# x loaded in two halves of 512 features, with the second half transposed behind the second slot of the first projection

## The chip, the core and the metric

The kernel runs on one core of a Trainium2 chip. The metric is device time in microseconds. The engines that this text speaks of are TensorE (PE in the profile), which multiplies; ScalarE (ACT), VectorE (DVE) and GpSimd (POOL), which prepare its operands; and SyncE (SP), which issues the loads. Each runs its own list of instructions in order, and they wait for one another by semaphores.

## What is computed

Two transformer blocks run one after the other on x, 512 tokens of 1024 features. Only the first lines of the first block lie near the change:

```python
def rms_norm(x, gain):
    xf = x.astype(jnp.float32)
    y = xf * lax.rsqrt(jnp.mean(xf * xf, axis=-1, keepdims=True) + EPS)
    return (y * gain.astype(jnp.float32)).astype(x.dtype)

hn = rms_norm(x, norm1_g[l])
proj = hn @ w_in[l]
qa, ka, va = [proj[..., i * WIDTH_A:(i + 1) * WIDTH_A] ... for i in range(3)]
...
x = x + mixed @ w_out[l]
x = x + conv_glu(rms_norm(x, norm2_g[l]), w_ffn_up[l], ...)
```

The projection `qa` sums over all 1024 features. The norm's root is taken of the mean of squares over all 1024 features too.

## The kernel before, in words

**Products in slots.** Every projection is cut into slots. A slot is one block of 128 input features (index k, eight of them in 1024) by 512 output columns. Its weights are one load of 128x512 fp32 into one of four raw buffers (`w_raw`, line 638). ScalarE rounds it to `w_hi` (`hi`, line 897) and GpSimd subtracts to get `w_lo` (`lo`, line 688); there are eight buffers of each. The activations are split likewise: `h_hi` by ScalarE (`first_unscaled`, line 941) and `h_lo` by VectorE (`first_lo`, line 1443). TensorE makes three products for each of four output tiles, twelve matmuls of 128x128 by 128x512 in a slot (line 1693; line 1715 for the first slot). The results of the first projection, qA, gather in banks 0 to 3 of the accumulation memory.

**Loads.** SyncE's queue issues them in order. The load of slot s waits until `w_lo` of slot s-4 is done (line 631 and the wait after it), since both halves of the split read the raw buffer. Behind the loads of slots 4 to 7 stand 18 small loads of gains and the like (lines 606 to 621), five behind each of the first three.

**The start.** x comes as four blocks of 128 tokens (`tb`) by 1024 features, 512 KB each, and then the weights of slots 0 to 3. TensorE transposes each block in eight pieces of 128x128 (`turned`, line 1748), so that feature block j of all tokens stands in bank j. For each j, VectorE or ScalarE copies the bank to `xT` (`first_copied`, lines 1435 and 934), ScalarE makes `h_hi` with the gain (the root is applied only to the outputs), and VectorE makes `h_lo`. ScalarE also squares and sums each block of tokens along the features (`first_square`, line 929), which gives one number per token and block in `xstat`.

**The sum of squares.** VectorE spreads each of the four columns of `xstat` over an identity matrix, in a rounded part and a rest (`sum_hi` line 1477, `sum_lo` line 1478, 128x128 each, eight instructions in all). The step `sumsq` is two matmuls of TensorE over them (lines 1651 and 1652). It stands behind slot 5 of qA in TensorE's order and waits for the last `sum_lo`. Then ScalarE takes the root (lines 952 and 954), and VectorE scales qA by it while copying out (line 1151).

**What sets the order.** `make_schedule` writes one list of steps by hand, and every engine runs through that list and does its part of each step. The number ahead of a step in the plan is the slot behind which it stands: `(5, ("sumsq", 0))`. A step `fill` is the splitting of a slot's weights eight slots ahead. `bank_uses` goes through the same list to count who used which bank before.

## Time and profile before

| | before |
|---|---|
| median of 3 runs | 1571.48 us (1570.23 to 1572.79) |
| span of the profiled execution | 1569.2 us |
| TensorE busy | 1559.0 us, 99% of the span |
| ScalarE busy | 692.7 us, 44% |
| VectorE busy | 643.8 us, 41% |
| GpSimd busy | 754.0 us, 48% |
| HBM traffic | 142.24 MB read, 2.13 MB written, 92 GB/s |

The profiled execution has no time of its own beside the span from its first to its last instruction; the median of the runs lies 2.3 us above that span. A busy share is an average over the whole span. The change touches some thirty microseconds at its start, so the rows further down are nearly all from there, and times in them are microseconds from the start of the span.

### The profile page before, as it was taken

To read this page: it belongs to the slowest core of one execution; us is meant where nothing else is said; L and a number is where in the kernel's file an instruction comes from. 1 tells how busy PE (TensorE), PEld (TensorE's weight loads), DVE (VectorE), ACT (ScalarE), POOL (GpSimd) and SP (SyncE) were. 2 spreads that over 40 slices of the span, in tenths; PEclk is the share of its full clock that TensorE was granted. 3 is DMA by queue.
4 is the path that set the end of the run, shared out by engine and by line. 5 is a ranking of instruction groups with operands and counts; after the bars stand their busy time and mean duration, and the time that the engine had idled before them with its cause. 6 is when DMAs were issued, how large, how long until landed. Compare 5 with 4: busy or idle time off the path is not lost.

```text
span 1569.2 us, 23311 instructions
## 1 busy us (share of the span) xinstructions
PE 1559.0 (99%) x8022; PEld 1258.1 (80%) x8022; DVE 643.8 (41%) x1081; ACT 692.7 (44%) x1194; POOL 754.0 (48%) x577
## 2 busy tenths in 40 slices
PE   8999999999999999999999999999999999999999
PEld 7877777888888888888877887778888888888887
DVE  5344465244355444220488544542442222210234
ACT  5565445334544444332543644754353333322342
POOL 6632475543644454444487433334544444444441
PEclk9999999999999999999999999999999999999999
DMA  5422222222323333333333224222333333333331
GB/s 178 149 74 62 67 68 68 83 86 88 115 86 95 107 100 99 96 97 92 81 95 90 76 66 135 68 68 75 108 94 101 95 99 94 113 95 98 96 94 61
DMA packets 103352, 145.60 MB, mean 93 GB/s; under 512 B 11109, under 2 KB 57166, under 8 KB 103134
## 3 DMA queue, kind: packets, MB, share of 16 engines
q1 hardware_dynamic: 103102, 142.30, 30.9%
q10 hardware_dynamic: 160, 2.11, 0.3%
q8 instruction: 55, 0.90, 0.2%
q14 instruction: 35, 0.29, 0.1%
HBM read 142.24 MB, written 2.13 MB: 92 GB/s over the span
## 4 chain that ended last, share of the span: by engine, by line
PE 97%; DVE 1%; DMA 0%; issue 0%; ACT 0%; SPq 0%; DVEq 0%; ACTq 0%
PE bank L1693 88%; PE bank L1601 2%; PE bank L1630 2%; PE bank L1618 2%; PE bank L1848 1%; DMA xtok<-in_x 0%; PE bank L1679 0%; DVE h_lo L1443 0%; PE bank L1871 0%; PE bank L1888 0%; PE bank L1748 0%; PE bank L1824 0%; PE bank L1882 0%; PE bank L1909 0%; PE bank L1825 0%
## 5 line engine op out<-in xcount | busy, mean ns | idle before, releaser
L688 POOL TENSOR_TENSOR w_lo<-w_raw,w_hi 128x512 fp32r<-128x512 f32 x516 | 697.6, 1361 | 784.8 <-ACT w_hi L897 784.2
L897 ACT ACTIVATE w_hi<-w_raw 128x512 fp32r<-128x512 f32 x516 | 320.0, 630 | 660.8 <-PE bank L1693 590.7
L1693 PE MATMUL bank<-h_hi,w_lo 128*128 128x512 f32 x1244 | 489.0, 393 | 1.5 <-DVE hgate L1159 1.4
L1693 PE MATMUL bank<-h_hi,w_hi 128*128 128x512 f32 x1244 | 484.4, 389 | 0.0
L1693 PE MATMUL bank<-h_lo,w_hi 128*128 128x512 f32 x1244 | 484.2, 389 | 0.0
L1693 PEld LDWEIGHTS bank<-h_hi,w_lo 128*128 128x128 f32 x1244 | 233.6, 188 | 52.8 <-issue 2.6
L1693 PEld LDWEIGHTS bank<-h_hi,w_hi 128*128 128x128 f32 x1244 | 233.5, 188 | 49.3
L1693 PEld LDWEIGHTS bank<-h_lo,w_hi 128*128 128x128 f32 x1244 | 233.7, 188 | 47.1
L1281 DVE TENSOR_TENSOR bank<-bank,rstd 128x512 f32<-128x512 f32 x88 | 60.1, 700 | 261.4 <-PE bank L1693 261.4
L1693 PE MATMUL bank<-g_hi,w_lo 128*128 128x512 f32 x352 | 137.0, 389 | 0.0
L1693 PE MATMUL bank<-g_hi,w_hi 128*128 128x512 f32 x352 | 136.9, 389 | 0.0
L1693 PE MATMUL bank<-g_lo,w_hi 128*128 128x512 f32 x352 | 136.9, 389 | 0.0
L1182 DVE TENSOR_TENSOR xT<-bank,xT 128x512 f32<-128x512 f32 x32 | 22.1, 689 | 205.7 <-PE bank L1693 203.4
L1693 PEld LDWEIGHTS bank<-g_hi,w_lo 128*128 128x128 f32 x352 | 66.1, 188 | 13.8
L1693 PEld LDWEIGHTS bank<-g_lo,w_hi 128*128 128x128 f32 x352 | 66.1, 188 | 13.7
L1693 PEld LDWEIGHTS bank<-g_hi,w_hi 128*128 128x128 f32 x352 | 66.1, 188 | 13.6
L1693 PE MATMUL bank<-w_lo,h_hi 128*128 128x512 f32 x184 | 73.5, 399 | 0.4 <-DVE fk L1156 0.4
L1693 PE MATMUL bank<-w_hi,h_hi 128*128 128x512 f32 x184 | 71.8, 390 | 0.0
L1693 PE MATMUL bank<-w_hi,h_lo 128*128 128x512 f32 x184 | 71.7, 390 | 0.0
L1290 DVE SCALAR_TENSOR_TENSOR acc<-bank,vec,acc 128x511 f32<-128x511 f32 x88 | 62.9, 746 | 13.3 <-ACT acc L852 8.1
L813 ACT ACTIVATE work<-work,mneg 128x128 f32<-128x128 f32 (+2 forms) x64 | 35.9, 561 | 37.7 <-DVEq L1264 36.9
L1693 PE MATMUL bank<-mix_hi,w_lo 128*128 128x512 f32 x128 | 49.8, 389 | 0.0
(297 smaller groups left out, 1769.6 us busy)
## 6 DMA issues: line engine op xcount, KB each, us to landing
w_raw<-in_w_in SPq DMA_DIRECT2D x168, 256.0 KB
w_raw<-in_w_ffn_up SPq DMA_DIRECT2D x88, 256.0 KB
w_raw<-in_w_ffn_down SPq DMA_DIRECT2D x88, 256.0 KB
w_raw<-in_w_ffn_gate SPq DMA_DIRECT2D x88, 128.0 KB
w_raw<-in_w_ffn_up SPq DMA_DIRECT2D x88, 128.0 KB
w_raw<-in_w_out SPq DMA_DIRECT2D x32, 256.0 KB
w_raw<-in_w_branch_a SPq DMA_DIRECT2D x16, 256.0 KB
w_raw<-in_w_branch_b SPq DMA_DIRECT2D x16, 256.0 KB
```

The source lines that it names most:

```text
L688: e.tensor_tensor(w_lo[:, pos % SPLIT_SLOTS, :], w_raw[:, pos % RAW_SLOTS, :], w_hi[:, pos % SPLIT_SLOTS, :].bitcast(F32), ALU.subtract).t ...
L813: ins = e.activation(ring, ring, ACT.Exp, scale=-1.0, bias=mneg[:, k, j:j + 1], accum_out=rsum[:, k, j:j + 1])
L897: e.activation(w_hi[:, pos % SPLIT_SLOTS, :], w_raw[:, r, :], ACT.Copy).then_inc(hi_full, 1)
L1182: e.tensor_tensor(xT[:, j, :], bank, xT[:, j, :], ALU.add).then_inc(x_ready, 1)
L1281: e.tensor_tensor(ps[banks + n][:, :], ps[banks + n][:, :], rstd[:, :], ALU.mult).then_inc(q["scaled"], 1)
L1290: e.scalar_tensor_tensor(out=o, in0=ps[banks + n][:, 0:S - shift], scalar=vec[:, conv_col(tap, col, n // 2)], in1=o, op0=ALU.mult, op1=ALU ...
L1601: mm = e.matmul(banks[h][:, at:at + n], qk1[qn][r, pair, qb * P:n], qk1[kn][r, pair, 0:n], start=True, stop=True)
L1618: mm = e.matmul(bank[64 * h:64 * h + 64, c * P:S], vtok[vn][:, c, d], probs_t[kind][:, h, c, c * P:S], start=c == 0, stop=c == TB - 1, ski ...
L1630: mm = e.transpose(bank[:, o:o + P], work[(2 * j + h) % 4][:, c * P:(c + 1) * P], ident[:, :])
L1693: mm = e.matmul(ps[banks + n][:, :], l, r, start=k == 0 and i == 0, stop=k == p.kc - 1 and i == 2)
L1848: mm = e.matmul(o, k_[:, h, k0:k0 + 32], q, start=True, stop=True, skip_group_check=True)
```

## The change

x is loaded as eight pieces of 128 tokens by 512 features, 256 KB each. The four pieces of the first half (feature blocks 0 to 3) come first, then the weights of slots 0 and 1, then the four pieces of the second half, then the weights of slots 2 and 3.

TensorE transposes the first half ahead of slot 0, into banks 4 to 7. A new step `turn` behind slot 1 transposes the second half into the same banks: 16 transposes that stood ahead of slot 0 before. Slot 0 no longer waits for copies of the banks, since qA writes to banks 0 to 3 and the transposes to banks 4 to 7; bank 0 holds the gains first, and slot 0 waits for their copy.

The squares are summed over half rows, in eight instructions where there were four, and VectorE adds the two halves. The eight instructions for `sum_hi` and `sum_lo` move behind the last `h_lo`. ScalarE and VectorE go through the copies and splits in another order. Some semaphores that nothing waited for are dropped.

```diff
+TURN = 1
...
-        [(5, ("sumsq", 0)), (5, ("rstd", 0)), (9, ("rtok", 0)), (8, ("vec", 1)), (13, ("masks",))]
+        [(TURN, ("turn",)), (5, ("sumsq", 0)), (5, ("rstd", 0)), (9, ("rtok", 0)), (8, ("vec", 1)), (13, ("masks",))]
...
         if x[0] == "start":
-            take(("vec", 0), 7)
-            for j in range(4, 8):
+            for j in range(4):
+                take(("x", j), 4 + j)
+        elif x[0] == "turn":
+            for j in range(4, DC):
                 take(("x", j), j)
         elif x[0] == "vec":
...
+            def load_x(tb, half):
+
+                c = slice(half * S, (half + 1) * S)
+                e.dma_start(xtok[:, tb, c], a["x"][0, tb * P:(tb + 1) * P, c]).then_inc(x_full[half][tb], 16)
+
             for tb in range(TB):
-                e.dma_start(xtok[:, tb, :], a["x"][0, tb * P:(tb + 1) * P, :]).then_inc(x_full[tb], 16)
+                load_x(tb, 0)
                 if tb == 0:
...
                             load(p.name, g, k, p.slot0 + g * p.kc + k)
+                            if p.name == "qA" and k == 1:
+                                for tb in range(TB):
+                                    load_x(tb, 1)
...
-            def first_square(tb):
-
-                e.wait_ge(x_full[tb], 16)
-                e.activation(x_squares[:, tb, :], xtok[:, tb, :], ACT.Square, accum_out=xstat[:, tb:tb + 1]).then_inc(x_sums, 1)
+            def first_square(tb, half):
+
+                e.wait_ge(x_full[half][tb], 16)
+                if half:
+                    e.wait_ge(x_sums, TB)
+                c = slice(half * S, (half + 1) * S)
+                e.activation(x_squares[:, tb, :], xtok[:, tb, c], ACT.Square, accum_out=xstat[:, half, tb:tb + 1]).then_inc(x_sums, 1)
 
             def first_copied(j):
 
                 e.wait_ge(xt_done, j + 1)
-                link(e.activation(xT[:, j, :], ps[j][:, :], ACT.Copy))
+                link(e.activation(xT[:, j, :], ps[4 + j][:, :], ACT.Copy))
+                e.nop().then_inc(bank_free[4 + j], 1)
                 e.nop().then_inc(x_last, 1)
 
             def first_unscaled(j):
 
-                if j != 3:
+                if j == 3:
+                    e.wait_ge(x_last, 1)
+                else:
                     e.wait_ge(x_rest, (0, 1, 2, 4, 5, 6, 7).index(j) + 1)
                 e.activation(h_hi[:, j, :], xT[:, j, :], ACT.Copy, scale=vec[:, j:j + 1]).then_inc(uhi_ready, 1)
 
                 if what == "start":
...
                     for tb in range(TB - 1):
-                        first_square(tb)
+                        first_square(tb, 0)
                     hi(0, 0)
                     e.wait_ge(gains_ready, 1)
                     first_unscaled(0)
+                    hi(1, 1)
+                    first_unscaled(1)
                     first_copied(3)
-                    for j in range(1, DC):
+                    first_unscaled(2)
+                    hi(2, 2)
+                    first_unscaled(3)
+                    first_square(TB - 1, 0)
+                    hi(3, 3)
+                    for tb in range(TB):
+                        first_square(tb, 1)
+                    for j in range(4, DC):
                         first_unscaled(j)
                         hi(j, j)
-                        if j == 4:
-                            first_square(TB - 1)
                 elif what == "fill":
...
-                    link(e.tensor_copy(vec[:, 0:8], ps[7][:, 0:8]))
-                    e.nop().then_inc(bank_free[7], 1)
+                    link(e.tensor_copy(vec[:, 0:8], ps[0][:, 0:8]))
                     e.nop().then_inc(gains_ready, 1)
                     e.wait_ge(const_ready, 1)
-                    for j in range(3):
+                    first_copied(0)
+                    first_copied(1)
+                    first_lo(0)
+                    first_copied(2)
+                    for j in range(1, 4):
+                        first_lo(j)
+                    for j in range(4, DC):
                         first_copied(j)
-                    for j in range(4):
                         first_lo(j)
-                        first_copied(4 + j)
-                    first_lo(4)
+                    e.wait_ge(x_sums, 2 * TB)
+                    link(e.tensor_tensor(xstat[:, 0, :], xstat[:, 0, :], xstat[:, 1, :], ALU.add))
                     for tb in range(TB):
-                        e.wait_ge(x_sums, tb + 1)
-
                         c = slice(tb * P, (tb + 1) * P)
-                        link(e.tensor_scalar(sum_hi[:, c], ident[:, :], xstat[:, tb:tb + 1], None, ALU.mult))
-                        ins = e.scalar_tensor_tensor(out=sum_lo[:, c], in0=ident[:, :], scalar=xstat[:, tb:tb + 1],
+                        link(e.tensor_scalar(sum_hi[:, c], ident[:, :], xstat[:, 0, tb:tb + 1], None, ALU.mult))
+                        ins = e.scalar_tensor_tensor(out=sum_lo[:, c], in0=ident[:, :], scalar=xstat[:, 0, tb:tb + 1],
                                                      in1=sum_hi[:, c].bitcast(F32), op0=ALU.mult, op1=ALU.subtract)
                     ins.then_inc(sum_lo_ready, 1)
-                    for j in range(5, DC):
-                        first_lo(j)
                     e.wait_ge(x_last, 1)
                     e.nop().then_inc(x_ready, DC)
                 elif what == "vec":
                 x_hi, x_lo = mixed[name[-1]] if name.startswith("out") else (h_hi, h_lo)
                 return x_hi[:, k, :], x_lo[:, k, :]
 
+            def turned(j, tb):
+
...
+            def turned(j, tb):
+
+                mm = e.transpose(ps[4 + j % 4][:, tb * P:(tb + 1) * P], xtok[:, tb, j * P:(j + 1) * P], ident[:, :])
+                if tb == TB - 1:
+                    mm.then_inc(xt_done, 1)
...
-                    def turned(j, tb):
-                        mm = e.transpose(ps[j][:, tb * P:(tb + 1) * P], xtok[:, tb, j * P:(j + 1) * P], ident[:, :])
-                        if tb == TB - 1:
-                            mm.then_inc(xt_done, 1)
-
                     for tb in range(TB):
-                        e.wait_ge(x_full[tb], 16)
-                        for j in range(DC - 1):
+                        e.wait_ge(x_full[0][tb], 16)
+                        for j in range(4):
                             turned(j, tb)
                         if tb == 0:
                             e.wait_ge(gain_full, 16)
-                            e.transpose(ps[7][:, 0:8], vrows[0:8, 0, :], ident[0:8, 0:8]).then_inc(vec_done, 1)
-                        if tb == 1:
-                            bank_wait(e, ("x", 7))
-                            turned(7, 0)
-                        if tb:
-                            turned(7, tb)
+                            e.transpose(ps[0][:, 0:8], vrows[0:8, 0, :], ident[0:8, 0:8]).then_inc(vec_done, 1)
                     e.wait_ge(const_dve, 2)
+                elif what == "turn":
+                    for tb in range(TB):
+                        e.wait_ge(x_full[1][tb], 16)
+                    for j in range(4, DC):
+                        bank_wait(e, ("x", j))
+                        for tb in range(TB):
+                            turned(j, tb)
                 elif what == "vec":
 
                     bank = bank_wait(e, x)
                     def check(n):
                         prev = previous_group(name, g)
...
                         if prev is None:
-                            if n == 3:
-                                e.wait_ge(x_last, 1)
-                            else:
-                                e.wait_ge(x_rest, n + 1)
+                            e.wait_ge(gains_ready, 1)
```

**VectorE's order.** These are the rows of VectorE's program before, from the copy of feature block 6 to the first copy-out of qA; the dots leave out the other six sums. COPY is `first_copied`, the 128x512 SCALAR_TENSOR_TENSOR is `first_lo`.

```order
L1435 COPY xT<-bank 128x512
L1443 SCALAR_TENSOR_TENSOR h_lo<-xT,vec,h_hi 128x512
L1435 COPY xT<-bank 128x512
L1443 SCALAR_TENSOR_TENSOR h_lo<-xT,vec,h_hi 128x512
L1477 TENSOR_SCALAR sum_hi<-ident,xstat 128x128
L1478 SCALAR_TENSOR_TENSOR sum_lo<-ident,xstat,sum_hi 128x128
...
L1443 SCALAR_TENSOR_TENSOR h_lo<-xT,vec,h_hi 128x512 x3
L1151 TENSOR_TENSOR qA<-bank,rstd 128x4x128 x4
```

And this is the changed program, from the copy of block 2; the dots leave out blocks 5 and 6 and the other six sums:

```order
L1464 COPY xT<-bank 128x512
L1471 SCALAR_TENSOR_TENSOR h_lo<-xT,vec,h_hi 128x512 x3
L1464 COPY xT<-bank 128x512
L1471 SCALAR_TENSOR_TENSOR h_lo<-xT,vec,h_hi 128x512
...
L1464 COPY xT<-bank 128x512
L1471 SCALAR_TENSOR_TENSOR h_lo<-xT,vec,h_hi 128x512
L1504 TENSOR_TENSOR xstat<-xstat 128x4
L1507 TENSOR_SCALAR sum_hi<-ident,xstat 128x128
L1508 SCALAR_TENSOR_TENSOR sum_lo<-ident,xstat,sum_hi 128x128
...
L1179 TENSOR_TENSOR qA<-bank,rstd 128x4x128 x4
```

Before, the copy of block j+4 stood behind the split of block j, and the sums stood between the splits of blocks 4 and 5. Now each of blocks 4 to 7 is copied and then split, one after the other, and all the sums stand behind the split of block 7.

**ScalarE's order.** Before, from the copy of block 3 on (ACTIVATE of `w_hi` is `hi`, of `h_hi` is `first_unscaled`):

```order
L934 ACTIVATE xT<-bank 128x512
L941 ACTIVATE h_hi<-xT,vec 128x512
L897 ACTIVATE w_hi<-w_raw 128x512
L941 ACTIVATE h_hi<-xT,vec 128x512
L897 ACTIVATE w_hi<-w_raw 128x512
L941 ACTIVATE h_hi<-xT,vec 128x512
L897 ACTIVATE w_hi<-w_raw 128x512
L941 ACTIVATE h_hi<-xT,vec 128x512
L897 ACTIVATE w_hi<-w_raw 128x512
L929 ACTIVATE x_squares,xstat<-xtok 128x1024
```

The changed program, from the same copy on:

```order
L952 ACTIVATE xT<-bank 128x512
L962 ACTIVATE h_hi<-xT,vec 128x512
L912 ACTIVATE w_hi<-w_raw 128x512
L962 ACTIVATE h_hi<-xT,vec 128x512
L947 ACTIVATE x_squares,xstat<-xtok 128x512
L912 ACTIVATE w_hi<-w_raw 128x512
L947 ACTIVATE x_squares,xstat<-xtok 128x512 x4
L962 ACTIVATE h_hi<-xT,vec 128x512
L912 ACTIVATE w_hi<-w_raw 128x512
```

The split of block 4 now stands behind the weights of slot 2, the weights of slot 3 and five squares.

## Rows read from the trace of the kernel before

**Rows 1.** The page, chain that ended last by engine; then PE's waits over the span.

```profile
PE 97%; DVE 1%; DMA 0%; issue 0%; ACT 0%; SPq 0%; DVEq 0%; ACTq 0%
...
PE bank L1748 <- DMA xtok<-in_x: 2.0, 1, 2.0
PE bank L1715 <- DVEq L1436: 1.0, 1, 1.0
```

**Rows 2.** The chain in order of time, first 60 us: start, us, what.

```profile
1.69 6.08 DMA xtok<-in_x
...
7.81 3.98 PE bank L1748 x19
...
12.62 0.72 ACT h_hi L941
...
27.67 0.76 DVE h_lo L1443
28.47 3.06 PE bank L1693 x12
```

**Rows 3.** Stretches: busy of PE, PEld, DVE, ACT, POOL; PE clock; DMA share; GB/s.

```profile
5.00:8.00 3.00, 0.97 (x9) 0.71 (x8) 0.17 (x1) 0.69 (x3) 0.00 (x0) 1.00 0.89 309
8.00:11.80 3.80, 3.80 (x21) 3.80 (x21) 0.03 (x1) 2.72 (x5) 0.09 (x1) 0.55 0.84 322
11.00:12.00 1.00, 1.00 (x9) 1.00 (x8) 0.23 (x1) 0.56 (x1) 0.29 (x1) 0.79 0.25 96
```

**Rows 4.** The tile xtok, its loads; then SP's timeline.

```profile
DMA to landing us min/median/max: 3.5/6.5/7.7
...
22.15 0.37 SPq L638 DMA_DIRECT2D w_raw<-in_w_in  x1
```

**Rows 5.** ACT's timeline: start, us, line, operation.

```profile
17.98 0.62 ACT L897 ACTIVATE w_hi<-w_raw 128x512 fp32r<-128x512 f32 x1
18.51 1.05 ACT L929 ACTIVATE x_squares<-xtok 128x1024 f32<-128x1024 f32 x1
19.55 0.71 ACT L941 ACTIVATE h_hi<-xT,vec 128x512 fp32r<-128x512 f32 x1
...
25.17 0.64 ACT L897 ACTIVATE w_hi<-w_raw 128x512 fp32r<-128x512 f32 x1 [1.11 <-DMA w_raw<-in_w_in]
```

**Rows 6.** DVE's timeline, copies and splits.

```profile
17.04 0.68 DVE L1435 COPY xT<-bank 128x512 f32<-128x512 f32 x1
17.96 0.86 DVE L1443 SCALAR_TENSOR_TENSOR h_lo<-xT,vec,h_hi 128x512 fp32r<-128x512 f32 x1 [0.24 <-DVE xT L1435]
18.74 0.68 DVE L1435 COPY xT<-bank 128x512 f32<-128x512 f32 x1
```

**Rows 7.** DVE's timeline, the sums.

```profile
22.16 1.31 DVE L1477 TENSOR_SCALAR sum_hi<-ident,xstat 128x128 fp32r<-128x128 f32 x1
23.50 1.46 DVE L1478 SCALAR_TENSOR_TENSOR sum_lo<-ident,xstat,sum_hi 128x128 fp32r<-128x128 f32 x1
24.88 0.28 DVE L1477 TENSOR_SCALAR sum_hi<-ident,xstat 128x128 fp32r<-128x128 f32 x1
25.20 0.35 DVE L1478 SCALAR_TENSOR_TENSOR sum_lo<-ident,xstat,sum_hi 128x128 fp32r<-128x128 f32 x1
...
26.05 1.32 DVE L1477 TENSOR_SCALAR sum_hi<-ident,xstat 128x128 fp32r<-128x128 f32 x1
27.40 0.35 DVE L1478 SCALAR_TENSOR_TENSOR sum_lo<-ident,xstat,sum_hi 128x128 fp32r<-128x128 f32 x1
```

**Rows 8.** POOL's timeline, 24 to 29 us.

```profile
23.52 1.29 POOL L688 TENSOR_TENSOR w_lo<-w_raw,w_hi 128x512 fp32r<-128x512 f32 x1
25.88 1.40 POOL L688 TENSOR_TENSOR w_lo<-w_raw,w_hi 128x512 fp32r<-128x512 f32 x1 [1.07 <-ACT w_hi L897]
```

**Rows 9.** PE's timeline, the step sumsq and its neighbour.

```profile
31.36 0.39 PE L1651 MATMUL bank<-sum_hi,mean_d 128*128 128x512 f32 x1
31.82 0.39 PE L1693 MATMUL bank<-h_hi,w_lo 128*128 128x512 f32 x1
```

More of the change, by code:

```diff
@@ L381, in two_block_kernel @@
         decay = place("decay", [P, HH, NH])
-        xstat = place("xstat", [P, TB])
+        xstat = place("xstat", [P, 2, TB])
         hstat = place("hstat", [P, TB, 3, HH])
@@ L405, in two_block_kernel @@
         xtok = u("xtok", 0, [P, TB, D])
-        x_squares = u("x_squares", 48, [P, TB, D])
+        x_squares = u("x_squares", 48, [P, TB, S])
         vrows = u("vrows", 16, [P, 3, P])
@@ L474, in two_block_kernel @@
         const_dve = sem("const_dve")
-        x_full = [sem(f"x_full{tb}") for tb in range(TB)]
+        x_full = [[sem(f"x_full{half}{tb}") for tb in range(TB)] for half in range(2)]
         gain_full = sem("gain_full")
@@ L494, in two_block_kernel @@
         A = {kind: {n: sem(f"{n}{kind}") for n in (
-            "sc_done", "s_ready", "e_ready", "r_ready", "p_ready", "tr_done", "pv_done", "yhi", "ylo")}
+            "sc_done", "s_ready", "p_ready", "tr_done", "pv_done", "yhi", "ylo")}
             for kind in "BAF"}
+        for kind in "AF":
+            A[kind] |= {n: sem(f"{n}{kind}") for n in ("e_ready", "r_ready")}
         A["B"] |= {n: sem(f"{n}B") for n in ("keep_ready", "beta_ready", "after_ready")}
@@ L499, in two_block_kernel @@
         up_sem = {n: {k: sem(f"{n}_{k}") for k in (
-            "scaled", "first", "conv1", "conv2", "silu", "prod", "hi", "lo")} for n in ("up1", "up2")}
+            "scaled", "first", "conv1", "silu", "prod", "hi", "lo")} for n in ("up1", "up2")}
         hgs = {n: sem(f"hg_{n}") for n in (
@@ L1434, in first_copied @@
                 e.wait_ge(xt_done, j + 1)
-                link(e.tensor_copy(xT[:, j, :], ps[j][:, :]))
+                bank = 4 + j % 4
+                link(e.tensor_copy(xT[:, j, :], ps[bank][:, :]))
                 e.nop().then_inc(x_rest, 1)
-                if j >= 4:
-                    e.nop().then_inc(bank_free[j], 1)
+                e.nop().then_inc(bank_free[bank], 1)
             def first_lo(j):
```

## The prediction, as it was put on record

> **What bounds the kernel now.** I read the chain of work that ended last first. TensorE holds 97% of it, and its waits over the whole span are few: 2.0 us for x, 1.0 us for the first copies [rows 1]. So the time is TensorE's work plus what it stands still, and only a change in standing still counts. The same chain in order of time shows where that is [rows 2]. Until 7.77 us it is the arrival of x (1.69 + 6.08), then the transposes, then a copy and a split, and TensorE only runs without gaps from about 17 us. The last piece of another engine in the chain is VectorE's split of block 5 at 27.67, which slot 5 waits for until 28.47. Behind slot 5 stands the sum of squares, at 31.36, and from there on TensorE runs at one matmul each 0.23 us (two from 31.36 to 31.82) [rows 9]. I use 31.36 as the mark: if the changed kernel starts this step D later or earlier, and nothing is lost or won after it, the kernel is D slower or faster. The reader should then look at what this step waits for.
>
> **Part one: TensorE starts earlier.** The first half of x is 1.05 MB, as much as blocks 0 and 1 of before, and block 1 had landed at 7.77 [rows 2]. At the 309 GB/s of the stretch from 5 to 8 us [rows 3], 1.05 MB take 3.4 us, which counted from 1.69 gives 5.1. A block's landing took 3.5 to 7.7 us from its issue [rows 4]. I take 7.0, between the two but nearer the landing that was seen. After the last piece come four transposes (0.4 us), a copy (0.68), a split by ScalarE (0.71) and some 0.3 us of handing on: slot 0 starts at 9.1 instead of 13.4 (12.62 + 0.72 and the handing on) [rows 2, 5, 6]. Slots 0 and 1 are 24 matmuls, 5.5 us at 0.23, with about 0.5 us of waits for their splits: 15.1. The 16 transposes of `turn` ran in 0.21 us each when the clock was low (19 in 3.98 us) [rows 2]; half of that, 0.105, is the floor at full clock; I take 0.125 each, 2.0 us: 17.1. Slots 2 to 5 are 48 matmuls, 10.9 us: TensorE reaches the sum of squares at 28.0, 3.4 us before the mark. This is the gain if nothing else holds it.
>
> The reads in half rows cost nothing that I can see. x's long rows moved at 309 GB/s from 5 to 8 us, the stretch from 8 to 11.8 us, which is mostly weights in 2 KB rows, at 322 [rows 3]. The Trainium skill speaks against the split (DMA: Bandwidth & Descriptors, Bandwidth): it wants loads of 1 MiB or more, and the fixed part of a load that it gives, about 2 us, would stand four times more. By the page alone that would be up to 8 us, by the rows nothing, since the loads queue behind one another and the engines are busy at 0.89 [rows 3].
>
> **Part two: the sum of squares comes later.** Follow ScalarE. All 3.15 MB of x and the first weights are in when the rate falls to 96 GB/s, between 11 and 12 us [rows 3], and the same bytes move in the changed kernel. Slot 2's weights are the last but one load: I take 11.6, bounds 10.8 and 12.9. ScalarE's next list is: weights 2 (0.53 from start to start, 17.98 to 18.51), split of block 3 (0.62), the last square of the first half, weights 3 (0.53), four squares of the second half, split of block 4. A full square takes 1.04 with its read of the sum (18.51 to 19.55); half of it, with the fixed part kept, is 0.62 [rows 5]. So the split of block 4 starts at 11.6 + 0.05 + 0.53 + 0.62 + 0.62 + 0.53 + 4 x 0.62 = 16.4. It also needs the copy of block 4, after `turn` has done its first four transposes at 15.6: 15.6 + 0.68 + 0.16 = 16.4 as well.
>
> Then a chain with no overlap, because each of blocks 4 to 7 is copied and split in turn: copy 0.68, hand over 0.16, ScalarE's split 0.71, hand over 0.08, VectorE's split 0.78 (17.96 to 18.74) [rows 5, 6]: 2.41 a block. Before, a block took 1.70 (17.04 to 18.74), the copies running ahead. VectorE ends the split of block 7 at 16.4 + 0.71 + 0.08 + 3 x 2.41 + 0.76 = 25.2. Slots 5 to 7 need theirs later than that (block 5's at 20.4 for 25.3), so this hides behind TensorE.
>
> The nine small instructions behind it don't. Look at the sums of before: 128x128 instructions that take 0.28 and 0.35 us at 24.88 and 25.20 took 1.31, 1.46 and 1.32 at 22.16, 23.50 and 26.05 [rows 7]. The first two and the last ran while GpSimd made `w_lo`; the short ones fell in GpSimd's gap between 24.81 and 25.88 [rows 8]. So each waits for one whole instruction of GpSimd, then GpSimd takes its turn: 1.40 us for each (22.16 to 24.96 for two). Before, three of eight were held, and the row took 5.6 us, all before 27.75. In the changed kernel the row starts at 25.3, just when `hi` of slot 7 and, right behind it, of slots 8 to 10 end (slot 7's at 25.0, each next 0.53 later). Their raw buffers were refilled meanwhile: a load is issued when the split four slots ahead is done and lands 3.0 us later (22.15 to 25.17) [rows 4, 5]. GpSimd therefore has `w_lo` of slots 7, 8, 9 and 10 at once and 11, 12 and 13 soon after, seven instructions. Bounds: none held, 9 x 0.32 = 2.9, ready at 28.2; three held as before, 3 x 1.40 + 6 x 0.3 = 6.0, 31.3; seven held, 10.4, 35.7. I take six, 6 x 1.40 + 3 x 0.3 = 9.3: ready at 34.6.
>
> The Trainium skill states the same lock (SBUF — State Buffer, "SBUF: two separate sides"): a VectorE instruction with two inputs there, or in a two-port mode, and a GpSimd one exclude each other for the whole instruction. By that rule the new 128x4 addition is held as well, which no row here shows; counted free or held, it moves my sum by 1.1 at most.
>
> **Part three: the clock.** TensorE stands from 28.0 to 34.6, 6.6 us. In the trace of before it stood 2.0 us until 7.81 [rows 1, 2], and from 8.0 to 11.8 its mean granted clock was 0.55 (nearly all of it at the 1.2 GHz level), though it was busy throughout [rows 3]. If the same follows this longer gap, 3.8 us at half rate lose 1.9 us. Bounds 0 and 1.9; I take 1.9, since the gap is three times as long. The same can befall slot 0 after the thin transposes; it would push block 4's copy back by up to 1.9 us.
>
> **The sum.** Start of the sum of squares 34.6 against 31.36: +3.2. Clock: +1.9. Together +5.1 on the profiled span, 1569.2 to 1574.3. The median stands 2.3 above that span, so 1571.5 + 5.1 = 1576.6 us. Nothing takes it back: qA's copies wait for the root some 2 us behind the step, and TensorE needs the first bank only two slots (5.4 us) later. A difference under 0.2% (3.1 us) is about what a measurement can't tell from no change.
>
> **Rivals.**
> - *The stall, without the clock's part.* With five held the step starts at 33.5 and with seven at 35.7, so +2.1 to +4.3: 1573.6 to 1575.8. For it: that a gap is followed by the low clock is known from one gap. Against it: that gap was shorter.
> - *Fewer are held.* With three held as before, the step starts at 31.3 and the time is 1571.4, or 1573.3 with the clock's part. For it: GpSimd ran dry in the same stretch of before, 1.07 us waiting for `hi` [rows 8], and ScalarE's `hi` was waiting for weights [rows 5]. Against it: at 25 us more weights have landed now.
> - *Faster.* The sums are ready when TensorE comes, at 28.2: 1571.5 - 3.2 = 1568.3, and 1567.5 if slot 2's weights land at 10.8 too. It needs all nine free; one held (28.2 + 1.1 = 29.3) leaves 2.1 us, which is under 0.2%. For it: the 3.4 us of part one don't depend on the lock. Against it: the row of before had three held with less of GpSimd's work ready.
> - *Worse.* Slot 0 at the low clock as well and seven held: 35.7 + 1.9, +6.2, and the second clock loss, +8.1: 1579.6.
>
> **How the numbers follow.** Forecast as summed, held five to seven with the clock's part: 0.42. Stall without clock: 0.15. Fewer held: 0.23. Faster: 0.12. Worse: 0.08. The time is that of the first, with +4.0 to +6.2, 1575.5 to 1577.7, as its own range. The range of all reaches from 1569.8 to 1579.3, leaving out most of the faster case and part of the worst. Slower by over 0.2%: 0.42 + 0.08 + half of the second = 0.57. Within 0.2%: the other half, the third, a little of the fourth: 0.32. Faster: 0.11.
>
> **What would show it.** Slot 0's first matmul near 9.1 instead of 13.44. The transposes of the second half near 15 to 17. The split of block 7 ending near 25.2. Sums of 1.2 to 1.5 us, six of nine. A gap of TensorE from 28 to nearly 35 with the sum of squares behind it, and a clock near 0.5 for some microseconds after. The prediction is wrong if the sums run at 0.3 us, if ScalarE gets block 4 much earlier because the loads finish earlier, or if TensorE comes to the step after 31 us, since then its own path decides.

## The result: 0.45% slower, with a 6.2 us stop of TensorE ahead of the sum of squares

| | before | after |
|---|---|---|
| median of 5 runs, same chip | 1570.92 us (1569.21 to 1572.79) | 1577.5 us (1576.39 to 1578.8) |
| ratio | 1 | 1.0045, 95% interval 1.0034 to 1.0056 |
| span of the profiled execution | 1569.2 us | 1575.8 us |

The chain of the changed kernel in order of time, against [rows 2]; start, us, what:

```profile
3.03 5.24 DMA w_raw<-in_w_in
...
9.75 4.47 PE bank L1749 x12
...
17.42 0.70 DVE xT L1464
...
18.21 0.73 ACT h_hi L962
...
25.58 0.75 DVE h_lo L1471
26.33 1.19 DVE xstat L1504
27.54 1.29 DVE sum_hi L1507
...
35.36 0.36 DVE sum_lo L1508
35.73 0.14 issue
35.86 0.77 PE bank L1685
```

Before, the chain was on TensorE from 28.47 on. Now it leaves TensorE at 17.42 and runs through the copies and splits of blocks 4 to 7 and then through the nine instructions of the sums, without a pause, to 35.72. Slot 0 does start earlier, at 9.75 instead of 13.4, and none of that is left. TensorE's waits over the span, against [rows 1]:

```profile
PE bank L1685 <- DVE sum_lo L1508: 6.2, 1, 6.2
PE bank L1749 <- ACT h_hi L962: 1.5, 1, 1.5
```

The 2.0 us for x and the 1.0 us for the first copies are gone, and 1.5 + 6.2 us have come. VectorE's timeline, against [rows 7] (start, us, then the idle time before in brackets):

```profile
24.04 0.69 DVE L1464 COPY xT<-bank 128x512 f32<-128x512 f32 x1
25.58 0.75 DVE L1471 SCALAR_TENSOR_TENSOR h_lo<-xT,vec,h_hi 128x512 fp32r<-128x512 f32 x1 [0.85 <-ACT h_hi L962]
26.25 1.26 DVE L1504 TENSOR_TENSOR xstat<-xstat 128x4 f32<-128x4 f32 x1
27.54 1.28 DVE L1507 TENSOR_SCALAR sum_hi<-ident,xstat 128x128 fp32r<-128x128 f32 x1
28.86 1.26 DVE L1508 SCALAR_TENSOR_TENSOR sum_lo<-ident,xstat,sum_hi 128x128 fp32r<-128x128 f32 x1
...
33.87 1.26 DVE L1508 SCALAR_TENSOR_TENSOR sum_lo<-ident,xstat,sum_hi 128x128 fp32r<-128x128 f32 x1
35.05 0.27 DVE L1507 TENSOR_SCALAR sum_hi<-ident,xstat 128x128 fp32r<-128x128 f32 x1
35.36 0.35 DVE L1508 SCALAR_TENSOR_TENSOR sum_lo<-ident,xstat,sum_hi 128x128 fp32r<-128x128 f32 x1
```

and GpSimd's beside it, against [rows 8]:

```profile
26.14 8.84 POOL L703 TENSOR_TENSOR w_lo<-w_raw,w_hi 128x512 fp32r<-128x512 f32 x7 [0.86 <-ACT w_hi L912]
```

GpSimd has seven `w_lo` in one piece, 26.14 to 34.98, and exactly the seven instructions of VectorE that start in it take 1.26 to 1.29 us. The two behind it take 0.27 and 0.35. Even the addition of 128x4, four numbers a row, took 1.26. The last rows are TensorE's, against [rows 9], and the stretch around them, against [rows 3] (the granted clock is the number behind the five busy times):

```profile
29.23 0.39 PE L1727 MATMUL bank<-h_hi,w_hi 128*128 128x512 f32 x1
35.86 0.77 PE L1685 MATMUL bank<-sum_hi,mean_d 128*128 128x512 f32 x1 [6.24 <-DVE sum_lo L1508]
36.43 0.63 PE L1686 MATMUL bank<-sum_lo,mean_d 128*128 128x512 f32 x1
36.85 0.63 PE L1727 MATMUL bank<-h_hi,w_lo 128*128 128x512 f32 x1
```

```profile
34.00:40.00 6.00, 4.14 (x10) 3.30 (x11) 1.68 (x3) 1.23 (x2) 0.98 (x1) 0.50 0.43 125
40.50:44.00 3.50, 3.50 (x17) 2.90 (x16) 1.92 (x3) 0.63 (x1) 1.30 (x1) 1.00 0.00 0
```

The sum of squares starts 4.5 us behind the mark of 31.36. Behind it the clock is at its 1.2 GHz level and the matmuls stand 0.42 to 0.43 us apart (36.43 to 36.85) instead of 0.23, until 40.27. Ten of them take 4.4 us (35.86 to 40.27) where they took 2.3 before (31.36 to 33.63): 2.1 us. The two together are the 6.6 us.

### The profile page after: what moved, and what is told of

It reads as the page before. It is cut to its first block, busy times and chain, and to the rows that moved or that the text cites. A ratio compares the mean times of both kernels' runs of the same rounds, so it can differ in the third digit from the quotient of the medians.

```text
span 1575.8 us, 23333 instructions
## 1 busy us (share of the span) xinstructions
PE 1561.0 (99%) x8022; PEld 1259.7 (80%) x8022; DVE 645.7 (41%) x1082; ACT 692.3 (44%) x1202; POOL 751.8 (48%) x577
## 4 chain that ended last, share of the span: by engine, by line
PE 97%; DVE 2%; DMA 0%; ACT 0%; issue 0%; SPq 0%; DVEq 0%
PE bank L1727 88%; PE bank L1629 2%; PE bank L1658 2%; PE bank L1646 2%; PE bank L1876 0%; PE bank L1713 0%; DMA w_raw<-in_w_in 0%; PE bank L1749 0%; PE bank L1899 0%; DVE sum_lo L1508 0%; PE bank L1916 0%; DVE sum_hi L1507 0%; PE bank L1852 0%; ACT h_hi L962 0%; PE bank L1910 0%; PE bank L1937 0%
```

## The experiments

In the tables and below, "before" is the kernel before on the same chip. Its median was 1569.98 us for the first four kernels, 1570.05 for the next four and 1569.42 for the last two.

**sums_early: the changed kernel with the sums ahead of block 4.**

```diff
                     for j in range(1, 4):
                         first_lo(j)
-                    for j in range(4, DC):
-                        first_copied(j)
-                        first_lo(j)
                     e.wait_ge(x_sums, 2 * TB)
...
                     ins.then_inc(sum_lo_ready, 1)
+                    for j in range(4, DC):
+                        first_copied(j)
+                        first_lo(j)
```

> The changed kernel with the addition and the eight sums moved ahead of the copy of block 4 on VectorE, nothing else. Theory (late sums held by GpSimd, then the low clock): the last square ends near 17.0 and GpSimd has nothing to do until 19.5, so all nine run free, 2.8 us, ready near 19.9. The copies and splits of blocks 4 to 7 come 2.5 us later, which slots 4 to 7 still allow. TensorE reaches the sum of squares near 29.5 and does not wait; no low clock after it. Time 8.4 us under the changed kernel and 1.9 under the kernel before: 1569. Rival (the loads in half rows, the moved transposes or the shared banks cost time by themselves): a loss against the kernel before stays, 1573 or more.

Measured: 1573.75 us, ratio 1.0023 (1.0013 to 1.0032). The expected 1569 was missed by nearly 5 us. The sums did what was expected: VectorE's timeline begins

```profile
17.21 0.17 DVE L1501 TENSOR_TENSOR xstat<-xstat 128x4 f32<-128x4 f32 x1 [2.31 <-ACT x_squares L947]
17.41 0.29 DVE L1504 TENSOR_SCALAR sum_hi<-ident,xstat 128x128 fp32r<-128x128 f32 x1
```

with all nine at their own length, and the sum of squares started at 28.89 without a wait (TensorE had stood 0.9 us before it, for the `w_lo` of slot 4). The loss is further on, in a wait that the trace of before has none of, and the chain shows what it hangs on:

```profile
PE bank L1727 <- DVE qA L1179: 3.3, 1, 3.3
```

```profile
28.46 3.85 POOL w_lo L703 x3
32.37 3.07 DMA w_raw<-in_w_in
...
35.46 0.63 ACT w_hi L912
36.09 0.49 ACT work L973
...
36.70 0.64 ACT rstd L975
...
37.43 0.70 DVE qA L1179
...
38.27 4.58 PE bank L1727 x12
```

TensorE needs qA's bank, VectorE copies it out with the root, and ScalarE's root (L973) stands in its list behind `hi` of slots 11 to 13, whose loads are late: that of slot 13 left only at 32.37, when GpSimd had done the `w_lo` of slots 7 to 9. The root started some 6.5 us after its operand was there (29.11 to 36.00, less 0.4 for the matmul). From 38.9 to 42.0 the granted clock was 0.54 as well. In the changed kernel this second wait is hidden: the root starts at 37.09, straight behind the late sum of squares. So the late sums were not the only thing that stood in the way of the earlier start.

**pool_held: the sums left late, GpSimd kept off them.** GpSimd waits for the last `sum_lo` ahead of `w_lo` of slot 7:

```diff
                     for s in range(SPLIT_SLOTS):
+                        if s == SPLIT_SLOTS - 1:
+                            e.wait_ge(sum_lo_ready, 1)
                         lo(s, s)
```

> The changed kernel, where GpSimd waits for the last sum_lo before it makes w_lo of slot 7; the sums stay where the change put them. Theory: the nine small instructions run free from 26.3 on, 2.9 us, ready near 29.2; TensorE comes at 29.5 and does not wait. w_lo of slot 7 is ready at 30.5, slot 7 needs it at 32.7. Time 1569, as with early sums. Rival (the place alone, each small instruction is long for a reason of its own, or waits for something of ScalarE): the sums take 1.25 us each as before, ready at 35.7, and the time stays at 1577.5.

Measured: 1573.46 us, ratio 1.0019 (1.001 to 1.0028): the time missed for the same reason (the sum of squares started at 28.48 without a wait, but the root only at 35.63, and TensorE waited 3.4 us for qA). The lock itself is settled. At the late place, behind the same split, VectorE's timeline is now

```profile
25.41 0.16 DVE L1506 TENSOR_TENSOR xstat<-xstat 128x4 f32<-128x4 f32 x1
25.60 0.28 DVE L1509 TENSOR_SCALAR sum_hi<-ident,xstat 128x128 fp32r<-128x128 f32 x1
```

and the nine take 2.6 us (25.41 to 28.03) instead of 9.5, with nothing else changed than that GpSimd doesn't run beside them.

**gap_filled: TensorE kept busy in its gap.** 24 matmuls stand ahead of the sum of squares; their results are not used.

```diff
                 bank = bank_wait(e, ("norm", norm))
+                if norm == 0:
+                    for i in range(24):
+                        e.matmul(bank[:, :], mean_d[:, :], h_hi[:, 0, :], start=True, stop=True)
                 e.wait_ge(sum_lo_ready, norm + 1)
```

> The changed kernel with 24 matmuls of 128x128 by 128x512 put ahead of the sum of squares on TensorE, into the bank that the sum of squares then writes afresh; they add no result. They take 5.4 of the 6.2 us for which TensorE stood. Theory: the stall stays as long (start of the sum of squares 35.9), the clock stays at its upper level, and the 2.0 us that the low clock cost are won: 1575.5. Rival (the long matmuls behind the stall are slow for another reason than the clock after a gap): 1577.5.

Measured: 1574.95 us, ratio 1.0032 (1.0019 to 1.0044), as expected. The stretches from 28.3 to 34 us, and from 35 us on:

```profile
28.30:34.00 5.70, 5.58 (x25) 4.30 (x23) 5.63 (x5) 1.90 (x3) 5.70 (x5) 1.00 0.74 212
35.00:40.00 5.00, 4.91 (x22) 4.07 (x23) 0.76 (x3) 1.86 (x3) 0.64 (x1) 1.00 0.28 82
```

The sum of squares is as late (35.09), but it is followed at the full clock, 22 matmuls in five microseconds where the changed kernel has ten in the four behind its gap. TensorE still stood 1.2 us. Ten matmuls from the step on take 2.4 us (35.09 to 37.48) instead of 4.4, so the clock's part of the loss is 2.0 us at this place. At TensorE's next transposes the two traces are 2.8 us apart (46.73 and 43.92), 0.8 by the earlier start of the step and 2.0 by the clock. The two spans differ by 2.2 (1575.8 and 1573.6), so 0.6 is lost again further on, where it was not followed up. The six runs have a mean granted clock of 0.999 or 1.000 each, the five of the changed kernel 0.997 or 0.998.

**whole_sums_late: the kernel before, with only its eight sums moved behind the split of block 7.**

```diff
                     first_lo(4)
+                    for j in range(5, DC):
+                        first_lo(j)
                     for tb in range(TB):
...
-                    for j in range(5, DC):
-                        first_lo(j)
```

> The kernel before with one part of the change alone: its eight sums moved behind the split of block 7, x whole. Theory: block 7 is split near 24.6 there, since the copies ran ahead, and GpSimd is short of weights until 27.4, so at most four are held: ready at 29 to 31, TensorE comes at 30.9. Time 1571 +- 0.7, no change. Rival (a late place is enough): ready only after 32, 1573 or more.

Measured: 1576.42 us, ratio 1.0041 (1.0027 to 1.0055), missed by 5 us. I had thought that the late place hurts only with x in halves. It doesn't need them:

```profile
25.11 1.32 DVE L1479 TENSOR_SCALAR sum_hi<-ident,xstat 128x128 fp32r<-128x128 f32 x1
...
32.77 1.28 DVE L1479 TENSOR_SCALAR sum_hi<-ident,xstat 128x128 fp32r<-128x128 f32 x1
34.09 0.35 DVE L1480 SCALAR_TENSOR_TENSOR sum_lo<-ident,xstat,sum_hi 128x128 fp32r<-128x128 f32 x1
```

```profile
24.57 9.40 POOL L688 TENSOR_TENSOR w_lo<-w_raw,w_hi 128x512 fp32r<-128x512 f32 x7 [0.59 <-ACT w_hi L897]
```

Again seven `w_lo` in one piece and seven held, TensorE waits 4.6 us and starts the sum of squares at 34.58, with the clock at 0.50 from 34.5 to 40. In the kernel before, the place of the sums alone costs 6.4 us, about what the whole change costs. That doesn't make it the only cost in the changed kernel: with the sums early again it got back only about 3 of its 6.6 us, because of the root (sums_early).

**early_root: sums_early, and the root's step moved in the plan.**

```diff
-        [(TURN, ("turn",)), (5, ("sumsq", 0)), (5, ("rstd", 0)), (9, ("rtok", 0)), (8, ("vec", 1)), (13, ("masks",))]
+        [(TURN, ("turn",)), (5, ("sumsq", 0)), (2, ("rstd", 0)), (9, ("rtok", 0)), (8, ("vec", 1)), (13, ("masks",))]
```

> Early sums, and the root moved on ScalarE ahead of the weight splits of slots 11 to 13 (in the plan from behind slot 5 to behind slot 2). Theory: with early sums the root came at 36.0, only because it stood behind the split of slot 13's weights, which waited for their load; TensorE then stood 3.3 us for the first copy of qA and had the low clock for some 4 us after it. With the root in front it starts near 29.9 and TensorE does not stand: 3.3 + 1.6 us under early sums, 1568.8, about 1 us under the kernel before. Rival (the wait for qA comes from VectorE or from the bank, not from the place of the root): no change from early sums, 1573.7.

Measured: 1569.29 us, ratio 0.9993 (0.9984 to 1.0002). The sum of squares stands at 29.71, ScalarE's root at

```profile
30.81 0.58 ACT L973 ACTIVATE work<-bank 128x512 f32<-128x512 f32 x1
```

and TensorE waits for qA no longer. This shows that the root's place was the second wait: some 4.5 us between this kernel and sums_early. Against the kernel before, 0.8 us are less than can be told from nothing.

**early_root_warm: early_root with five small matmuls, whose results are not used, between and behind the first transposes.**

```diff
+WARM = (1, 1, 0, 3)
...
                             turned(j, tb)
+                        for i in range(WARM[tb]):
+                            e.matmul(ps[1][:, 0:P], mean_d[:, :].bitcast(F32), mean_d[:, :].bitcast(F32), start=True, stop=True)
```

> The same, with five small matmuls (128x128, ten passes) put between and behind the transposes of the first half on TensorE, written to a bank that slot 0 writes afresh. The low clock at the start came in some profiled executions and not in others (slot 0 took 4.3 us in the changed kernel, 3.2 in early sums). Theory: the matmuls keep the clock up, so slot 0 always takes the short time: 0 to 1 us under early_root, 1568.3. Rival (the clock at the start has nothing to do with the standing before it): as early_root, or the time of the matmuls later.

Measured: 1569.1 us (11 runs, 1568.9 to 1569.52), ratio 0.9994 (0.9985 to 1.0003). Slot 0 began at 10.20 at the full clock, and the sum of squares stood at 29.18. In the median nothing can be told from early_root, though its runs lie closer together (early_root: 1568.82 to 1570.28). The low clock at the start comes and goes between executions, as the last section shows, so one profile of each doesn't show that the five matmuls keep it away. Ten of its eleven runs have a mean granted clock of 1.000, against eight of eleven of early_root: too few to tell.

**copies_ahead: sums_early, with each copy of a bank ahead of the split before it.**

```diff
+                    first_copied(4)
                     e.wait_ge(x_sums, 2 * TB)
...
                     for j in range(4, DC):
-                        first_copied(j)
+                        if j + 1 < DC:
+                            first_copied(j + 1)
                         first_lo(j)
```

> Early sums behind the copy of block 4, the root where the change has it, and on VectorE the copy of block j+1 ahead of the split of block j, as before. Theory: the blocks 5 to 7 follow at 1.5 us instead of 2.2, so the weight splits of slots 5 to 7 and, through the raw buffers, the load of slot 13 come about 2 us earlier; the root starts near 34 instead of 36.0 and TensorE's gap is 1.3 us instead of 3.3, with no low clock after it: 3.6 us under early sums, 1570.1. Rival (slot 13's load is bound by the rate of the loads or by the queue's small loads, not by the chain of copies): root at 36, 1573.7.

Measured: 1572.61 us, ratio 1.002 (1.0011 to 1.0029). 1.1 us under sums_early, where 3.6 were expected. The shorter chain of blocks brought the root forward from 36.00 to 34.81, and the wait for qA shrank from 3.3 to 2.4 us. So only part of the root's lateness comes from that chain; behind it ScalarE's `hi` waits for the loads of slots 11 to 13 (0.7 to 1.7 us each in this trace). The other part of the miss is the clock. The expectation counted on no low clock behind the shorter gap, and the profiled execution has none, but it is the only one of the eleven with a mean granted clock of 1.000, at 1570.76 us. The other ten have 0.997 to 0.999 and took 1572.35 to 1574.47.

**whole_half_loads: the kernel before with each load of x cut in two halves, in the same order.** Both signal the same semaphore, and who waited for 16 waits for 32.

```diff
-                e.dma_start(xtok[:, tb, :], a["x"][0, tb * P:(tb + 1) * P, :]).then_inc(x_full[tb], 16)
+                for half in range(2):
+                    c = slice(half * S, (half + 1) * S)
+                    e.dma_start(xtok[:, tb, c], a["x"][0, tb * P:(tb + 1) * P, c]).then_inc(x_full[tb], 16)
```

> The kernel before with each of its four loads of x cut into two of 256 KB and 512 features, all in the order of before. Both halves are still waited for. Theory: the size of the loads costs nothing that can be measured, 1570 +- 0.7. Rival (smaller loads have a price of their own, as the rule on large loads has it): 1 to 8 us more.

Measured: 1570.88 us, ratio 1.0009 (1.0 to 1.0018), sum of squares at 30.55. That is 0.8 us ahead of the trace of before, which had the low clock at its start and this one not, so the two traces don't compare the loads. Loads of 256 KB cost 1.4 us by the ratio (0.8 by the medians), 0 to 2.8 by its interval, which just reaches no change.

**root_alone and sums_wide: two tests of how many are held.** root_alone has early_root's line alone; the sums stay late. sums_wide makes the eight sums in three instructions of 128x512:

```diff
-                    for tb in range(TB):
-                        c = slice(tb * P, (tb + 1) * P)
-                        link(e.tensor_scalar(sum_hi[:, c], ident[:, :], xstat[:, 0, tb:tb + 1], None, ALU.mult))
-                        ins = e.scalar_tensor_tensor(out=sum_lo[:, c], in0=ident[:, :], scalar=xstat[:, 0, tb:tb + 1],
-                                                     in1=sum_hi[:, c].bitcast(F32), op0=ALU.mult, op1=ALU.subtract)
-                    ins.then_inc(sum_lo_ready, 1)
+                    spread = x_squares[:, 0, :]
+                    link(e.tensor_tensor(spread.rearrange("p (t c) -> p t c", t=TB),
+                                         ident[:, :].rearrange("p (o c) -> p o c", o=1).broadcast_to([P, TB, P]),
+                                         xstat[:, 0, :].rearrange("p (t o) -> p t o", o=1).broadcast_to([P, TB, P]), ALU.mult))
+                    link(e.tensor_copy(sum_hi[:, :], spread))
+                    e.tensor_tensor(sum_lo[:, :], spread, sum_hi[:, :].bitcast(F32), ALU.subtract).then_inc(sum_lo_ready, 1)
```

> The changed kernel with the root's step moved in the plan from behind slot 5 to behind slot 2, and the sums left at the late place. On ScalarE the root then stands ahead of `hi` of slots 11 to 13 and waits there for the sum of squares, so GpSimd finds only the `w_lo` of slots 7 to 10 beside the sums, four instructions where it found seven. If a sum is held once for each instruction that GpSimd has ready (my theory), the addition and the first three sums are held at 1.27 us each, the last five take 0.27 to 0.35 us, the sums are ready near 33.0 instead of 35.7, and the time is about 2.7 us under the changed kernel's, 1574.8. If the root is just hidden behind the wait for the sums and the number of held instructions is set by something else (the rival), the time stays at 1577.5.

> The changed kernel with its eight 128x128 instructions for the sums made as three of 128x512 at the same late place: the four columns spread over the identity in one product, its rounding, and the rest. If the price is one turn of GpSimd for each instruction, however short it is (my theory), the four instructions (the addition and three long ones) cost about 1.3 us for the addition and 1.0 plus 0.7 for each long one, some 6.5 us instead of 9.5: ready near 32.7, and about 3 us under the changed kernel, 1574.5. If the price goes by the elements or by the time in which GpSimd is busy (the rival), the row of sums still lasts until GpSimd's seventh instruction is done, near 36 or later since the long instructions hold GpSimd up too, and the time is 1577.5 or more.

Measured for root_alone: 1574.56 us, ratio 1.0028 (1.0017 to 1.0038). VectorE's and GpSimd's timelines:

```profile
26.86 1.26 DVE L1504 TENSOR_TENSOR xstat<-xstat 128x4 f32<-128x4 f32 x1
...
30.67 1.28 DVE L1507 TENSOR_SCALAR sum_hi<-ident,xstat 128x128 fp32r<-128x128 f32 x1
31.98 0.35 DVE L1508 SCALAR_TENSOR_TENSOR sum_lo<-ident,xstat,sum_hi 128x128 fp32r<-128x128 f32 x1
```

```profile
26.76 5.11 POOL L703 TENSOR_TENSOR w_lo<-w_raw,w_hi 128x512 fp32r<-128x512 f32 x4 [0.86 <-ACT w_hi L912]
```

Four `w_lo`, four held, five free, as expected. The sums end at 33.50 and TensorE waits 3.4 us instead of 6.2. One of the nine runs took 4748.53 us, and no trace shows why; the ratio is that of the other eight.

Measured for sums_wide: 1573.07 us, ratio 1.0024 (1.0014 to 1.0034), 1.4 us better than expected. Its timelines:

```profile
25.13 1.26 DVE L1504 TENSOR_TENSOR xstat<-xstat 128x4 f32<-128x4 f32 x1
26.42 1.74 DVE L1506 TENSOR_TENSOR x_squares<-ident,xstat 128x512 f32<-128x512 f32 x1
28.20 1.37 DVE L1509 CAST sum_hi<-x_squares 128x512 fp32r<-128x512 f32 x1
29.60 1.64 DVE L1510 TENSOR_TENSOR sum_lo<-x_squares,sum_hi 128x512 fp32r<-128x512 f32 x1
```

```profile
25.03 9.82 POOL L703 TENSOR_TENSOR w_lo<-w_raw,w_hi 128x512 fp32r<-128x512 f32 x7 [0.86 <-ACT w_hi L912]
```

Three instructions cover the same outputs, with one pass more over them, and the row lasts 6.1 us (25.13 to 31.24) instead of 9.5. It is done 3.6 us before GpSimd's seventh, so it doesn't wait for GpSimd to run dry. The price is one turn of GpSimd for each instruction.

## Why the prediction was right, step by step

The forecast was 1576.6 us, the time 1577.5, and the forecast's mechanism is the one that the traces show. Its nearness is in part luck. The span grew by 6.6 us where 5.1 were forecast, and the time came out only 0.9 off because the forecast started from 1571.5, the median of three runs, where that of five is 1570.92. Its steps:

| step | forecast | measured |
|---|---|---|
| slot 0 starts | 9.1 | 9.75 |
| TensorE reaches the sum of squares | 28.0 | 29.46 (29.23 + 0.23) |
| split of block 4 starts | 16.4 | 18.21 |
| a block of the chain | 2.41 | 2.20 (18.21 to 20.41) |
| split of block 7 ends | 25.2 | 26.33 |
| held instructions of nine | 6, at 1.40 | 7, at 1.26 (8.80 from the first start to the eighth) |
| sums ready | 34.6 | 35.72 |
| the clock's part | 1.9 | 2.1 |
| on the span | +5.1 | +6.6 |

**The start.** Slot 0 was taken too early because its weights, not x, came last, and the sum had no term for them: their load lands at 8.27, and `hi` and the split of block 0 follow one another (8.30, 8.93). Slot 0 then ran at the low clock. Here is the stretch from 10 to 13 us in the changed kernel, and below it in gap_filled, whose slot 0 started at the same time (9.80):

```profile
10.00:13.00 3.00, 3.00 (x8) 2.32 (x9) 2.76 (x4) 2.67 (x6) 2.13 (x3) 0.51 0.97 361
10.00:13.00 3.00, 2.99 (x13) 2.14 (x13) 2.76 (x4) 2.37 (x5) 2.07 (x2) 1.00 0.97 368
```

Slots 0 and 1 took 7.0 us (9.75 to 16.79) instead of 5.8 (9.80 to 15.64): 1.2 us for the clock. The prediction named this as possible and gave it to its worst rival, together with seven held, at 1.9 us; both came, and the time is between that rival's 1579.6 and the forecast. With the 0.65 us by which slot 0 was late, it put the transposes of the second half 1.7 us later than forecast (16.79 for 15.1), which is most of the 1.8 on block 4's split. ScalarE's own list was done with the squares at 17.03, where 16.4 was forecast, so TensorE's transposes and the copy behind them set the time of that split. From there the chain ran as it was worked out, and a little faster.

**The sums.** The count was mis-sized by one, and the length of each was over-priced by 0.14 us. The two nearly cancel: 9.5 us for the row (26.25 to 35.72) against 9.3. The row started about 1 us later, and the step came 1.3 us later than forecast, at 35.86. pool_held, root_alone and sums_wide show the rule behind it. The Trainium skill has the lock (SBUF — State Buffer, "SBUF: two separate sides"), and the rows agree, also for the addition of 128x4, which the prediction had left open: 1.26 us in the changed kernel, 0.17 in sums_early, 0.16 in pool_held.

**The clock.** gap_filled shows that it is a part of the loss by itself: nearly the same late step, the full clock behind it, and 2.0 us less there, of which 1.4 are left at the end of the span. The count of slow matmuls in the changed kernel gives 2.1.

**Nothing takes it back** held for this kernel: TensorE waits for qA nowhere in it. But as a statement on what comes next it was incomplete. "TensorE needs the first bank only two slots (5.4 us) later" is right for the changed kernel only because the late sum of squares holds TensorE back too. With the sums in time, the root is the next that is late, 3.3 us. That is why my experiments' expectations of 1569 were missed where the prediction was not.

**The gain that the change could have had** was over-priced. The prediction said 3.4 us before the mark; kernels without the stall reached the step at 28.48 to 29.71. The kernel before reached it at 31.36 with the low clock at its start and, cut into half loads, at 30.55 without. So 1.4 to 2.1 us are there: with the low clock 31.36 against 29.46 (where TensorE arrives in the changed kernel) and 29.71, without it 30.55 against 28.48 to 29.18. Slot 0 starts 3.7 us earlier (9.75 against 13.44), but the transposes of the second half, which TensorE did ahead of slot 0 before, partly while it would have waited anyway, now stand between slots and take 1.66 us there (16.79 to 18.45). early_root, with both late steps mended, is at 0.9993 (0.9984 to 1.0002). The rival *Faster* had a slip as well: its 1567.5 puts the step at 27.4, ahead of the 28.0 at which the same prediction lets TensorE arrive, so 1568.1 was the least it could give.

The Trainium skill wants loads of 1 MiB or more (DMA: Bandwidth & Descriptors, "Bandwidth"); with the fixed part of about 2 us a load that the same page gives ("Anatomy of one DMA — SWDGE (gpsimd) path"), the prediction's estimate from the page was up to 8 us for the split alone. whole_half_loads doesn't bear that out: 0 to 2.8 us.

## What to carry to other kernels

Small VectorE instructions like these sums are cheap only where GpSimd has nothing to do. Before moving a row of them, look at how many instructions GpSimd has ready there: as many of the row are held, each for a whole one of GpSimd's, so place the row early, make fewer and longer instructions of it, or leave GpSimd short of work. And when TensorE's start is brought forward, follow every step that its later slots need (here the sums, then the root in ScalarE's list) and ask which loads stand ahead of it, since the loads don't come earlier with it.

## What the runs showed that I had not expected

**Turns, one for one.** The number of held instructions equals the number of GpSimd's in its unbroken piece: 7 and 7 in the changed kernel, in gap_filled and in whole_sums_late, 4 and 4 in root_alone, 1 and 1 in copies_ahead (19.09), none in pool_held. That is so where the row starts with the piece; in the kernel before it started near the end of a piece of six and met only the last two. GpSimd doesn't notice the short ones: seven of its instructions with them took 8.84 us, 1.26 each, and five without them in pool_held 6.28, 1.26 each too. Three long ones and the addition lengthen its seven to 9.82.

**The low clock after a stop is likely, not certain.** Stops of TensorE of 6.2, 4.6, 3.4, 3.3 and 3.3 us (the changed kernel, whole_sums_late, root_alone, sums_wide, sums_early) were each followed by a stretch at the 1.2 GHz level; one of 3.4 us (pool_held) and one of 2.4 us (copies_ahead) were not, in the executions that were profiled. The stretch of pool_held behind its stop:

```profile
38.00:42.00 4.00, 4.00 (x19) 3.01 (x20) 1.96 (x5) 0.68 (x2) 2.10 (x2) 1.00 0.66 167
```

The other runs show that these two profiles are the rarer case of their kernels. Of the eleven runs of pool_held four have a mean granted clock of 1.000 (1571.33 to 1572.37 us) and seven 0.998 or 0.999 (1572.89 to 1574.9): their medians lie 1.8 us apart. All ten of sums_early are below 1.000, and all but one of copies_ahead. The mean over a run doesn't say where in it the clock was low.

At the start it varies as well. In the profiled executions of before, the changed kernel, early_root and root_alone the clock was low for 3 to 4 us somewhere between 8 and 14 us, and in the eight others it was 1.00 from 8 to 14, though most of them run the same instructions up to there. What decides it is open.
